# First small projections and first attention projection of a hybrid decoder layer: work for tokens 0 to 511 placed between the transposes of tokens 640 to 1023

## The reference

```python
def reference(x, norm_mix, w_in, conv_w, a_log, dt_bias, dn_norm, ...):
    h = x
    u = rmsnorm(h, norm_mix[layer])
    proj = u @ w_in[layer]                       # (1024, 10768)
    qa, ka, va, qd, kd, vd, z, beta_raw, a_raw, gate_raw = jnp.split(proj, split_at, axis=-1)
    # A: dilated sliding-window softmax attention of qa, ka, va: 12 heads of 128 in three groups
    ...
    # B: gated delta rule of qd, kd, vd with, per token and each of 8 heads,
    beta = jax.nn.sigmoid(beta_raw)
    g = -jnp.exp(a_log[layer]) * jax.nn.softplus(a_raw + dt_bias[layer])
    ...
    h = h + (gate_a * y_a + gate_b * y_b) @ w_out[layer]
    h = h + (jax.nn.silu(hn @ w_gate[layer]) * (hn @ w_up[layer])) @ w_down[layer]   # hn = rmsnorm(h, ...)
    return rmsnorm(h, norm_final)
```

## Time and profile before

| | us |
|---|---|
| median of 3 runs (lowest, highest) | 2283.48 (2283.16, 2284.0) |
| profiled execution, whole | 2284.89 |
| its span | 2283.2 |
| TensorE busy in the span | 2208.1 (97%) |
| mean granted TensorE clock | 0.989 |

### The profile page before, as it was taken

One profiled execution on the slowest core, in us unless ns is written; L12 is line 12 of the kernel. 1 busy time (PEld: TensorE's weight loads), 2 busy tenths in 40 slices (PEclk: granted clock), 3 DMA queues, 4 the chain that ended last, 5 costly groups with the idle time before them and its releaser, 6 DMA issues.

```text
span 2283.2 us, 30688 instructions
## 1 busy us (share of the span) xinstructions
PE 2208.1 (97%) x11040; PEld 1834.1 (80%) x11040; DVE 1118.1 (49%) x1559; ACT 934.0 (41%) x1595; POOL 695.9 (30%) x529
## 2 busy tenths in 40 slices
PE   6899999999999999999999999999999999999997
PEld 5688787887887888888888887888788888878886
DVE  7522322323247656655655534425866666640153
ACT  5544344444444546555655542123533333320012
POOL 6686566566522111111111114331000000043340
PEclk8999999999999999999999999999999999999998
DMA  5111312213232201211221334251222222261221
GB/s 131 49 47 47 102 49 74 84 47 85 70 98 65 65 27 55 64 37 46 64 59 33 129 139 129 65 139 28 74 82 83 82 83 82 76 219 49 93 56 74
DMA packets 251922, 175.66 MB, mean 77 GB/s; under 512 B 41448, under 2 KB 225960, under 8 KB 251840
## 3 DMA queue, kind: packets, MB, share of 16 engines
q1 hardware_dynamic: 221776, 136.46, 20.5%
q10 hardware_dynamic: 30064, 38.10, 5.3%
HBM read 143.36 MB, written 31.18 MB: 76 GB/s over the span
## 4 chain that ended last, share of the span: by engine, by line
PE 86%; DVE 4%; issue 2%; ACT 2%; DMA 2%; POOL 1%; ACTq 1%; DVEq 1%; POOLq 1%; SPq 0%
PE bank L213 20%; PE bank L2261 16%; PE bank L1064 15%; PE bank L2523 10%; PE bank L1273 6%; PE bank L1523 2%; PE bank L1506 2%; PE bank L689 1%; PE bank L2277 1%; PE bank L1513 1%; PE bank L700 1%; PE bank L1560 1%; DVE own_sum_t L486 1%; PE bank L1555 1%; PE bank L1556 1%
## 5 line engine op out<-in xcount | busy, mean ns | idle before, releaser
L213 PE MATMUL bank<-u_hi,w_hi 128*128 128x512 f32 x704 | 311.3, 442 | 6.2 <-ACT z_next L1740 4.9
L199 POOL CAST w_hi<-raw 128x1024 fp32r<-128x1024 f32 (+1 forms) x60 | 62.4, 1040 | 726.3 <-PE bank L213 511.0
L213 PE MATMUL bank<-u_hi,w_lo 128*128 128x512 f32 x704 | 277.0, 393 | 0.0
L213 PE MATMUL bank<-u_lo,w_hi 128*128 128x512 f32 x704 | 276.0, 392 | 0.0
L2483 POOL CAST dn_hi<-dn_raw 128x896 fp32r<-128x896 f32 (+1 forms) x24 | 27.6, 1152 | 563.1 <-DMA dn_raw<-in_w_down 458.1
L213 PEld LDWEIGHTS bank<-u_hi,w_lo 128*128 128x128 f32 x704 | 132.4, 188 | 29.3
L213 PEld LDWEIGHTS bank<-u_hi,w_hi 128*128 128x128 f32 x704 | 133.8, 190 | 22.1 <-ACT z_next L1740 5.3
L201 POOL TENSOR_TENSOR w_lo<-raw,w_hi 128x1024 fp32r<-128x1024 f32 (+1 forms) x60 | 148.5, 2475 | 8.6
L213 PEld LDWEIGHTS bank<-u_lo,w_hi 128*128 128x128 f32 x704 | 134.1, 190 | 14.9 <-issue 1.9
L941 POOL TENSOR_TENSOR q_lo_s<-q_sum_s,q_hi_s 128x512 fp32r<-128x512 f32 x92 | 122.7, 1339 | 64.8 <-ACT q_hi_s L996 59.0
L1808 DVE SCALAR_TENSOR_TENSOR conv_out<-conv_in,conv_c,conv_out 128x1024 f32<-128x1024 f32 (+1 forms) x96 | 100.3, 1045 | 14.9 <-issue 12.0
(11 more groups left out here) (432 smaller groups left out, 5924.9 us busy)
## 6 DMA issues: line engine op xcount, KB each, us to landing
raw<-in_w_in SPq DMA_DIRECT2D x36, 512.0 KB, 3.9
raw_first<-in_w_in SPq DMA_DIRECT2D x24, 512.0 KB, 3.9
raw_second<-in_w_in SPq DMA_DIRECT2D x24, 512.0 KB, 4.6
row<-scr_rows ACTq DMA_DIRECT2D x24, 512.0 KB, 4.6
raw_gate<-in_w_gate SPq DMA_DIRECT2D x22, 512.0 KB, 4.0
raw_up<-in_w_up SPq DMA_DIRECT2D x22, 512.0 KB, 3.9
scr_v<-gate_out SPq DMA_DIRECT2D x44, 256.0 KB, 2.1
tmp<-scr_gate ACTq DMA_DIRECT2D x16, 512.0 KB, 3.5
```

The costliest lines, as they stand in the source:

```text
L199: nc.gpsimd.tensor_copy(hi[:, 0:kt, :], raw[slot][:, 0:kt, :])
L213: last = nc.tensor.matmul(bank[dst][:, :], wpart[slot][wp][:, k, :], rhs[ap][:, k, half * HALF:(half + 1) * HALF], start=k == 0 and (wp, a ...
```

## The change

On TensorE the small projections of tokens 0 to 511 stand behind the transposes of chunk 4, and the 16 steps of the first attention pair for tokens 0 to 511 behind the transposes of chunks 5 (4 steps), 6 (4) and 7 (8). The small projections of the other half, and the pair's 16 steps for it, follow behind the last transpose. The four results of the pair get four PSUM banks and come in another order (query and key of the first half, query and key of the second half), so that parts a and c are free for q = 1 at a count of 6 of `done`, not 4. GpSimd makes the low parts of u's first four chunks, then those of the four weight parts, then those of the last four chunks. ScalarE casts the weight parts between chunks 3 and 4, counted by a semaphore of their own (`ba_turned` is used for it, whose later waits are 4 higher). For q = 1 ScalarE casts s1, s2, a, c, s3 in this order (before: a, c, s1, s2, s3), and GpSimd's low parts wait for these counts.

```diff
@@ -281,2 +281,3 @@
         x_load = [sem(f"x_load{i}") for i in range(KT)]
+        first_high = ba_turned
@@ -352,3 +353,5 @@
-            for c in range(KT):
+        def row_lows(pool, t_half):
+            g = nc.gpsimd
+            for c in range(4 * t_half, 4 * t_half + 4):
                 for q in range(2):
@@ -422,5 +425,6 @@
                     roots(1)
+                elif c == 3:
+                    for name in ("a", "c", "b", "d"):
+                        part_high(act, 0, name)
-            for name in ("a", "c", "b", "d"):
-                part_high(act, 0, name)
             operand_cast(act, "t1")
@@ -511,7 +515,13 @@
                     last.then_inc(x_turned, 1)
-            pe.wait_ge(ba_split, 1)
-            for half in range(2):
-                pe.wait_ge(x_low, KT * (half + 1))
-                for k in range(KT):
-                    beta_decay(half, k)
+                if c == 4:
+                    pe.wait_ge(ba_split, 1)
+                    pe.wait_ge(x_low, KT)
+                    for k in range(KT):
+                        beta_decay(0, k)
+                elif c >= 5:
+                    for j in {5: range(4), 6: range(4, 8), 7: range(8, 16)}[c]:
+                        first_step_pe(pe, j)
+            pe.wait_ge(x_low, 2 * KT)
+            for k in range(KT):
+                beta_decay(1, k)
@@ -555,3 +565,3 @@
                 for c in (2 * (j - 56), 2 * (j - 56) + 1):
-                    act.wait_ge(ba_turned, c + 1)
+                    act.wait_ge(ba_turned, 4 + c + 1)
                     f(per_token[:, c, :, :], bank[X0 + c % 2][:, 0:P].rearrange("p (k e) -> p k e", e=32)[:, :, 0:8],
@@ -893,4 +903,4 @@
         FIRST_PART_AT = {"a": 1, "c": 2, "b": 3, "d": 7}
-        FIRST_FREE = {"a": 4, "c": 4, "s4": 7, "d": 7}
-        FIRST_OUT = (("a", "c", 0), ("a", "c", 1), ("b", "d", 0), ("b", "d", 1))
+        FIRST_FREE = {"a": 6, "c": 6, "s4": 7, "d": 7}
+        FIRST_OUT = (("a", "c", 0, D1), ("b", "d", 0, D0), ("a", "c", 1, X0), ("b", "d", 1, X1))
         q_hi["b"], q_lo["b"] = q_hi["s4"], q_lo["s4"]
@@ -939,3 +949,6 @@
             def low(name, src):
-                pool.wait_ge(qp["high"], HIGH_BEFORE + 7 * q + (HIGH_AT if q else FIRST_PART_AT)[name])
+                if q:
+                    pool.wait_ge(qp["high"], HIGH_BEFORE + 7 * (q - 1) + (HIGH_FIRST if q == 1 else HIGH_AT)[name])
+                else:
+                    pool.wait_ge(first_high, ("a", "c", "b", "d").index(name) + 1)
                 g.tensor_tensor(q_lo[name][:, :, :], src, q_hi[name][:, :, :].bitcast(F32),
@@ -980,2 +993,3 @@
         HIGH_AT = {"a": 1, "c": 2, "s1": 3, "s2": 4, "s3": 5, "s4": 6, "d": 7}
+        HIGH_FIRST = {"s1": 1, "s2": 2, "a": 3, "c": 4, "s3": 5, "s4": 6, "d": 7}
         HIGH_STEP = {1: ("a",), 2: ("c",), 4: ("s1", "s2"), 5: ("s3",), 6: ("s4",)}
@@ -995,4 +1009,3 @@
                 act.wait_ge(qp["done"], 7 * (q - 1) + BEFORE[name] + 1)
-            nc.scalar.activation(q_hi[name][:, :, :], src, ACT.Copy).then_inc(
-                qp["high"], 4 if q == 0 and name == "d" else 1)
+            nc.scalar.activation(q_hi[name][:, :, :], src, ACT.Copy).then_inc(qp["high"] if q else first_high, 1)
@@ -1012,11 +1025,14 @@
+            if j >= 16:
+                first_step_pe(pe, j)
+
+        def first_step_pe(pe, j):
+
             o, k = j // 8, j % 8
-            low_part, high_part, half = FIRST_OUT[o]
+            low_part, high_part, half, place_ = FIRST_OUT[o]
             name = low_part if k < 4 else high_part
-            if k % 4 == 0:
+            if k % 4 == 0 and half == 0:
                 pe.wait_ge(qp["part"], FIRST_PART_AT[name])
-                if k == 0:
-                    wait(pe, qp["copied"], o - 1)
             for wp, ap in PASSES:
-                last = nc.tensor.matmul(bank[D1 - half][:, :], (q_hi, q_lo)[wp][name][:, k % 4, :],
+                last = nc.tensor.matmul(bank[place_][:, :], (q_hi, q_lo)[wp][name][:, k % 4, :],
                                         act_in[ap][:, k, half * HALF:(half + 1) * HALF],
@@ -1031,3 +1047,3 @@
             o = j // 8
-            half = o % 2
+            half, place_ = FIRST_OUT[o][2:]
             act.wait_ge(qp["done"], (2, 4, 6, 7)[o])
@@ -1036,8 +1052,7 @@
                 act.wait_ge(x_low, 2 * KT)
-            nc.scalar.activation(qk_t[0][o // 2][:, half * HALF:(half + 1) * HALF], bank[D1 - half][:, :], ACT.Copy,
-                                 scale=1.0 if o // 2 else float(P) ** -0.5).then_inc(qp["copied"], 1)
-            if o == 1:
+            nc.scalar.activation(qk_t[0][o % 2][:, half * HALF:(half + 1) * HALF], bank[place_][:, :], ACT.Copy,
+                                 scale=1.0 if o % 2 else float(P) ** -0.5).then_inc(qp["copied"], 1)
+            if o == 2:
                 part_high(act, 1, "a")
                 part_high(act, 1, "c")
-            elif o == 2:
                 part_high(act, 1, "s3")
@@ -2673,5 +2688,8 @@
             setup_pool(pool, then)
+            row_lows(pool, 0)
             for q in range(NQ):
                 attention_pool(pool, q)
-                if q == 1:
+                if q == 0:
+                    row_lows(pool, 1)
+                elif q == 1:
                     sides_pool(pool, then)
```

## The result

The changed kernel takes 2290.81 us (median of 8 runs, 2288.36 to 2292.9), the kernel before in the same comparison 2285.06 (8 runs, 2283.16 to 2291.12). The ratio is 1.0024 with a 95% interval of 1.0014 to 1.0035: 5.5 us slower (3.2 to 8.0). The forecast was 8.4 us, 2291.9.

A forecast was written before the change was run, and what follows sets the result against it. TensorE, busy 97% of the span, was taken as the bound, its third product of q = 1 waiting for VectorE's t2. Late sums (4.6 us) plus a longer chain (3.8) gave 8.4 on 2283.48: 2291.9 us, 8-in-10 range 2286.5 to 2296.0.

The forecast's parts named there:

- The two causes: Setup: sums end 4.6 us late because u is late, and the chain from sums to t2 grows 3.8 us.
- the place named: TensorE's third product of q = 1, waiting for t2's low part: start at 88.8 us and not 80.34.
- TensorE's order delays u: Setup transposes behind small projections and matmuls: u done about 47.6, 10.6 us late; TensorE itself 1.8 us ahead.
- the bounds of the clock: TensorE ahead of u or at the third product: one half-clock stretch more or less, 1.7 us either way.
- The sums get faster: VectorE's sixteen sums with GpSimd less busy: 14.5 us, ending at 62.2, 4.6 us late.
- The chain gets longer: Sums to t2: a and c cast later, GpSimd's low parts ahead of s1's and s3; adds 3.8 us.
- Sum at the third product: TensorE's third product of q = 1: 4.6 + 3.8 = 8.4 us late.
- To the end: Behind the third product engines follow each other as before; all 8.4 us carried to the end.
- the small-loss rival: Behind the third product: slack gives half back, 4 us left, 2287.5 us; chance 0.16.
- the faster case: Setup: t2 ready by 80.24, needing sums done by 53.8; at most 6 us gained, 2277.5; chance 0.06.
- Met throughout: VectorE and GpSimd meet in all sums, 26.4 us: end at 2303.8, partly 2295.9; chance 0.13.
- the change does not do what it says: TensorE's small projections still start near 35.9, u_lo being late: 4.7 us on top, 2296.6; chance 0.05.

The follow-up runs named there:

- The second profile: The changed kernel run and profiled again, unaltered, against the kernel before: ratio 1.0037 (1.0025 to 1.0049), 2292.11 us median of 6.
- Experiment 4: Changed kernel with all TensorE transposes first, then the small projections and pair steps; against the kernel before 1.0026 (1.0015 to 1.0037).
- Experiment 3: Changed kernel with a and c of q = 1 cast early, behind the first pair's second copy; against the kernel before 1.0015 (1.0007 to 1.0024).
- two profiles of before: The kernel before, profiled first and then again unaltered; the repeat's ratio 0.9995 (0.9986 to 1.0004).
- experiment 6: Kernel before with ScalarE's cast of s3 of q = 1 moved behind the logarithms of the decay rows; 1.0004 (0.9995 to 1.0013).
- experiment 5: Changed kernel with both all transposes first and a and c cast early; against the kernel before 1.0008 (0.9999 to 1.0016).

## Why the prediction was right

The two causes and their order of size were right, and the loss came at the place named. That the time was met within 1.1 us (2291.9 for 2290.81) is partly luck: the loss was put at 8.4 us and measured as 5.5, and the forecast started from 2283.48, the median of 3 runs, where the 8 runs beside the changed kernel had 2285.06.

- *TensorE's order delays u*: right. The transposes, the end of u (47.6 forecast, 47.64) and the lead of 1.8 us at the end of the first pair came as worked out. The second profile had u 1.1 us later, by a longer stretch at the half clock; that is inside the bounds of the clock. Experiment 4 takes this cause away, and the sums start at 37.28.
- *The sums get faster*: right in size (14.5 us, end at 62.2 forecast, 62.20). The loads landed later than I had them: GpSimd's sums began at 56.76, not 53.8, which changes nothing, as they meet two of VectorE's sums wherever they stand. The Trainium skill's page "SBUF — State Buffer", section "Who interferes with whom", states that such a pair contends for an exclusive lock. My estimate from it, 1.95 us a pair, was not seen here either: no sum took over 1.78 us, and the stretches fit with 1.65 for a pair.
- *The chain gets longer*: right in kind, 2.9 us and not 3.8. The exponentials were released 0.7 us sooner (1.21 us for the step at L583, now alone, where it had taken 1.94 beside GpSimd), and GpSimd's four instructions followed each other every 1.22 to 1.24 us, not every 1.28. This is the term that was mis-sized. Experiment 3 takes it back.
- *Sum at the third product*: 8.4 forecast, 7.4 in the trace and 8.5 in the second profile, 1.1 of it by the clock ahead of u. The start at the full clock, which I had in the bounds, came true and gave 1.6 us. It was lost again by q = 2 to the wait for va_t and to the decay rows, whose longer wait behind ScalarE's `per_token` I had not named. That the second product would fall to the half clock (5.3 us for 3.0) I had not named either; it stood in the shadow of t2. I had said that behind the third product all engines follow at the same distance; they did so only from q = 2 on, and, in both profiles, at 7.0 to 7.4 us from 716 to 1350 us.
- *To the end*: the timed loss is 5.5 us in one comparison and 8.5 in the other. 8.4 lies just above the first interval (8.0) and inside the second. That time is given back late, as the small-loss rival says, was seen in one profile of two, which ended 8.0 us late even so, and has no cause that I could show.
- The rivals: the faster case needed the sums by 53.8 and had them at 62.2. "Met throughout" did not happen. That the change does not do what it says is out by the start at 31.01.

## What to carry to other kernels

Filling an idle stretch of the bound engine is worth only what its next wait does not take back. Here the work moved forward was worth 1.8 us, and stood ahead of transposes on which the longest chain of the setup hung: follow that chain through every engine before moving anything in front of its source. When the order of casts is changed to fit, look at what the helper engine has standing in its own queue behind them. And where two engines contend, a shorter chain on one can lengthen the other's: read the durations again at the new places.

## What the runs showed of the hardware

- VectorE's sums of two inputs in SBUF took 1.65 us each beside GpSimd's subtractions (13.19 us for eight in the kernel before, no single one of either kernel over 1.78) and 0.66 to 0.69 alone. In the meetings with the scan the engine whose instruction began second lost the time. The scan of 8 rows by 1024 took 2.28 us where it began ahead of GpSimd's low part (75.78 and 76.10, kernel before), and that low part took 5.29 us. It took 3.20 us where it began inside a GpSimd instruction (73.78, inside 73.10 to 74.83, experiment 6), and the GpSimd instruction behind it, started at 75.00, took 5.30 us.
- Across a wait of 0.97 to 1.11 us TensorE went from a second product at the half clock (0.43 us a matmul) to a third at the full one: from the third to the fourth product it was 2.84 us in the changed kernel (87.76 to 90.60), 2.85 in its second profile and 2.86 and 2.80 in experiments 3 and 4. Behind a wait of 1.87 us in experiment 5 and of 3.51 and 3.52 in the two profiles of before the same twelve matmuls ran mostly at the half clock: 4.42, 4.41 and 4.41 us. The length of the wait alone does not decide. In experiment 3 the first product of q = 1 (72.13) ran at 0.23 us a matmul throughout behind a wait of 3.21 us that followed the whole first pair. The second (78.63), behind 3.51 us, ran at 0.43. In the changed kernel the third product came 7.4 us late and ran 1.6 us faster; a lateness can be smaller behind a product than ahead of it.
